# Products of two output tiles in turn, behind the in-projection of a two-layer hybrid decoder step

## What is computed

```python
def hybrid_layer(x, ...):
    z = rmsnorm(x, g_mix) @ w_in                 # 2048 -> 5632, 11 projections of 512
    ...                                          # conv module, short conv, RG-LRU, retention
    mix = concat([y_a, y_b, y_c, y_d])
    x = x + mix @ w_out                          # 2048 -> 2048
    h2 = rmsnorm(x, g_ffn)
    gpre = causal_dwconv(h2 @ w_ffn_gate, ...)   # 2048 -> 5632, width 3
    x = x + (silu(gpre) * (h2 @ w_ffn_up)) @ w_ffn_down
```

## Time and profile before

| | us |
|---|---|
| median of 3 runs | 2357.85 |
| lowest, highest | 2357.66, 2360.24 |
| the profiled execution, its own time | 2360.99 |
| its span, first to last instruction | 2359.2 |

### The profile page before, as it was taken

The page is one execution under the profiler, slowest core; times in us unless marked ns, Lnnn a source line. Parts: engine busy times, 40 slices in busy tenths (PEclk is TensorE's granted clock), DMA queues, the critical chain, the costliest instruction groups (busy, mean ns, idle before and its releaser), DMA issues.

```text
span 2359.2 us, 44193 instructions
## 1 busy us (share of the span) xinstructions
PE 2306.2 (98%) x18830; PEld 2295.7 (97%) x18830; DVE 1620.6 (69%) x2581; ACT 1016.9 (43%) x1124; POOL 0.2 (0%) x4
## 2 busy tenths in 40 slices
PE   7999989999999999999999999999999999999997
PEld 7999989999999999999999998999999999999996
DVE  7987766666666666666789867557666666666666
ACT  6433644434433433433554346444433443443444
POOL 0000000000000000000000000000000000000000
PEclk9999999999999999999999999999999999999998
DMA  7646445555555555555566554455555555555552
GB/s 273 204 167 206 143 159 185 179 188 181 181 166 195 180 182 185 182 172 188 176 201 205 166 188 153 164 179 185 181 181 186 181 171 188 178 185 188 179 180 91
DMA packets 119237, 426.07 MB, mean 181 GB/s; under 512 B 15489, under 2 KB 15745, under 8 KB 119041
## 3 DMA queue, kind: packets, MB, share of 16 engines
q1 hardware_dynamic: 111888, 407.15, 52.5%
q10 hardware_dynamic: 7152, 16.09, 1.9%
HBM read 413.71 MB, written 9.48 MB: 179 GB/s over the span
## 4 chain that ended last, share of the span: by engine, by line
PE 94%; DVE 4%; DVEq 1%; ACT 1%; issue 0%; DMA 0%; SPq 0%; ACTq 0%
PE bank L560 31%; PE bank L561 31%; PE bank L562 30%; DVE wl L772 1%; PE bank L680 1%; DMA x<-in_x_in 0%; ACT wh L254 0%; PE bank L708 0%; PE bank L673 0%; DVE x L1218 0%; DVE u L801 0%; DVE ml L862 0%; DVE x L1168 0%; DVE ssq L1016 0%; PE bank L638 0%
## 5 line engine op out<-in xcount | busy, mean ns | idle before, releaser
L254 ACT ACTIVATE wh<-raw 128x1024 fp32r<-128x1024 f32 x768 | 813.0, 1062 | 1247.0 <-PE bank L562 1226.6
L560 PE MATMUL bank<-xh,wh 128*128 128x264 f32 x4224 | 1206.9, 286 | 13.3 <-DVE wl L772 10.9
L561 PE MATMUL bank<-xl,wh 128*128 128x264 f32 x4224 | 1200.4, 284 | 0.0
L562 PE MATMUL bank<-xh,wl 128*128 128x264 f32 x4224 | 1199.4, 284 | 0.0
L772 DVE TENSOR_TENSOR wl<-raw,wh 128x1024 fp32r<-128x1024 f32 x768 | 916.9, 1220 | 36.3 <-ACT wh L254 9.3
L560 PEld LDWEIGHTS bank<-xh,wh 128*128 128x128 f32 x4224 | 799.2, 189 | 17.5 <-issue 11.5
L561 PEld LDWEIGHTS bank<-xl,wh 128*128 128x128 f32 x4224 | 799.8, 189 | 0.4
L562 PEld LDWEIGHTS bank<-xh,wl 128*128 128x128 f32 x4224 | 795.6, 188 | 0.0
L560 PE MATMUL bank<-mh,wh 128*128 128x264 f32 x1920 | 548.3, 286 | 25.5 <-DVE ml L862 15.8
L561 PE MATMUL bank<-ml,wh 128*128 128x264 f32 x1920 | 547.6, 285 | 0.0
L562 PE MATMUL bank<-mh,wl 128*128 128x264 f32 x1920 | 544.7, 284 | 0.0
(11 more groups left out here) (196 smaller groups left out, 676.3 us busy)
## 6 DMA issues: line engine op xcount, KB each, us to landing
raw<-in_weights SPq DMA_DIRECT2D x768, 512.0 KB, 4.0
s_own<-in_ret_state ACTq DMA_DIRECT2D x4, 512.0 KB, 6.3
k<-in_ret_state ACTq DMA_DIRECT2D x4, 512.0 KB, 4.5
out_new_ret_sample<-s_own ACTq DMA_DIRECT2D x4, 512.0 KB, 5.5
out_new_ret_sample<-k ACTq DMA_DIRECT2D x4, 512.0 KB, 5.3
x<-in_x_in SPq DMA_DIRECT2D x3, 528.0 KB, 9.2
dg<-in_ffn_state ACTq DMA_DIRECT2D x2, 528.0 KB, 4.4
out_new_ffn_sample<-dg ACTq DMA_DIRECT2D x2, 528.0 KB, 2.7
```

The lines of the kernel that those rows point to most:

```text
L254: act.activation(wh[:, i, :], raw[:, i, :], ACT.Copy).then_inc(hi_made, 1)
L560: pe.matmul(out, w_hi, rh, start=first, stop=False)
L561: pe.matmul(out, w_hi, rl, start=False, stop=False)
L562: return pe.matmul(out, w_lo, rh, start=False, stop=last)
```

## The change

In the output projection (g = 12 to 14), up 0 and all gate and up groups of the loop, `group` is replaced by `group_by_twos`: two tiles, in two banks, go together, block by block, each of the three products for the one and then for the other. It uses two chunks at a time (the host puts the weights in that order) and needs four chunks for the two tiles, which end together. In-projection, groups in halves and down-projections stay. The waits on `chunk_used` and the arguments of `lows_to` follow: `4 * (m // 2) + 4` chunks in place of `2 * m + 2`, and for every second tile 2 chunks more. `silu_gate` on ScalarE goes one chunk earlier in the loop, and for block 0 behind the last chunk of the plan.

```diff
--- before.py
+++ after.py
@@ -90,8 +90,11 @@
 def done(p):
 
 
+
     g, m = divmod(p, 4)
-    return 8 * g + (5 + m if g in HALVES else 2 * m + 2)
+    if g in HALVES:
+        return 8 * g + 5 + m
+    return 8 * g + (2 * m + 2 if g < G_IN else 4 * (m // 2) + 4)
 
 
 class Signal:
@@ -490,20 +493,21 @@
                          (44, h_store_par)]
                 plan += [(43, h_mix(3 + m, 12 + m, 1, u[:, m, :], "yb", m + 1)) for m in range(4)]
                 plan += [(44 + kk, lambda kk=kk: h_x(kk)) for kk in range(KT)]
-                plan += [(61, lambda: std_of(l, 1)), (64, lambda: silu_gate(l, 0))]
+                plan += [(61, lambda: std_of(l, 1))]
                 plan.sort(key=lambda item: item[0])
                 for n in range(RING, 8 * G_LOOP):
                     hi(l * CHUNKS + n)
                     while plan and done(plan[0][0]) + LEAD <= n:
                         plan.pop(0)[1]()
                 assert not plan
+                silu_gate(l, 0)
 
                 for blk in range(1, NBLK):
                     for n in range(24):
                         hi(l * CHUNKS + G_LOOP * 8 + (blk - 1) * 24 + n)
                         if 8 <= n < 12:
                             hh_of(l, blk - 1, (blk - 1) % 2, n - 8)
-                        if n == 18:
+                        if n == 17:
                             silu_gate(l, blk)
 
                 def split_next(j):
@@ -580,6 +584,26 @@
                     for f in (hooks or {}).get(m, ()):
                         f()
 
+            def group_by_twos(chunk, i, tile, rh, rl):
+
+                for m in (0, 2):
+                    for j in range(2):
+                        c = 2 * m + 2 * j
+                        pe.wait_ge(lo_made, chunk + (c + 2))
+                        for b in range(8):
+                            kk = 8 * j + b
+                            at, cols = [(i + c + n) % RING for n in range(2)], slice(b * P, (b + 1) * P)
+                            for n in range(2):
+                                if kk == 0:
+                                    pe.wait_ge(bank_empty.sem, tile + (m + n + 1))
+                                pe.matmul(bank[:, m + n, 0:T], wh[:, at[n], cols], rh[:, kk, :], start=kk == 0, stop=False)
+                            for n in range(2):
+                                pe.matmul(bank[:, m + n, 0:T], wh[:, at[n], cols], rl[:, kk, :], start=False, stop=False)
+                            for n in range(2):
+                                last = pe.matmul(bank[:, m + n, 0:T], wl[:, at[n], cols], rh[:, kk, :], start=False, stop=kk == 15)
+                                if b == 7:
+                                    last.then_inc(chunk_used.sem, 1)
+
             def group_in_halves(chunk, i, tile, rh, rl, hooks=None, before=None):
 
                 for j in range(2):
@@ -732,12 +756,12 @@
                         on("mix_lo", l, kk - 8)
                 group_in_halves(c0 + G_IN * 8, G_IN * 8, t0 + G_IN * 4, mh, ml, None, mixers_ready)
                 for g in range(G_IN + 1, G_GATE0):
-                    group(c0 + g * 8, g * 8, t0 + g * 4, mh, ml)
+                    group_by_twos(c0 + g * 8, g * 8, t0 + g * 4, mh, ml)
                 group_in_halves(c0 + G_GATE0 * 8, G_GATE0 * 8, t0 + G_GATE0 * 4, xh, xl, {1: [lambda: sum_squares(1)]},
                                 norm_ready(l * 32 + KT))
 
                 on("std", l, 2)
-                group(c0 + G_UP0 * 8, G_UP0 * 8, t0 + G_UP0 * 4, xh, xl)
+                group_by_twos(c0 + G_UP0 * 8, G_UP0 * 8, t0 + G_UP0 * 4, xh, xl)
 
                 def hidden_ready(base):
                     def f(kk):
@@ -747,8 +771,8 @@
                 for blk in range(1, NBLK):
                     i = G_LOOP * 8 + (blk - 1) * 24
                     tb = t0 + G_LOOP * 4 + (blk - 1) * 8
-                    group(c0 + i, i, tb, xh, xl)
-                    group(c0 + i + 8, i + 8, tb + 4, xh, xl)
+                    group_by_twos(c0 + i, i, tb, xh, xl)
+                    group_by_twos(c0 + i + 8, i + 8, tb + 4, xh, xl)
                     down(c0 + i + 16, i + 16, l * PAIRS + (blk - 1) * 8, (blk - 1) % 2,
                          hidden_ready(l * (4 * NBLK) + (blk - 1) * 4))
                 down(c0 + G_LAST * 8, G_LAST * 8, l * PAIRS + (NBLK - 1) * 8, 0,
@@ -1121,7 +1145,7 @@
                     p = 44 + kk
                     dve.wait_ge(chunk_used.sem, chunk_used.at(l, done(p)))
                     tt(x[:, kk, :], x[:, kk, :], bank[:, p % 4, 0:T], ALU.add).then_inc(bank_empty.sem, 1)
-                    lows_to(c0 + done(p) + LEAD)
+                    lows_to(c0 + done(p) + LEAD + (0 if kk < 4 or kk == KT - 1 else 2 * (kk % 2)))
                     if kk:
                         split_x(l, 0, kk - 1, gain(1))
                     if kk == KT - 1:
@@ -1131,7 +1155,7 @@
                 add_squares(3, S["x_sq"].at(l, 4), e)
 
                 def gate_tile(chunk, m, last=None):
-                    dve.wait_ge(chunk_used.sem, chunk + ((last or 2 * m + 2) + RING))
+                    dve.wait_ge(chunk_used.sem, chunk + ((last or 4 * (m // 2) + 4) + RING))
                     tt(q[:, m, :], bank[:, m, 0:T], rs[:, :], ALU.mult).then_inc(bank_empty.sem, 1)
 
                 def gate_conv(f0, between=lambda: None):
@@ -1150,7 +1174,7 @@
                         between()
 
                 def up_tile(chunk, blk, m):
-                    dve.wait_ge(chunk_used.sem, chunk + (2 * m + 2 + RING))
+                    dve.wait_ge(chunk_used.sem, chunk + (4 * (m // 2) + 4 + RING))
                     tt(one_tile[m % 2], bank[:, m, 0:T], rs[:, :], ALU.mult).then_inc(bank_empty.sem, 1)
                     dve.drain()
                     if m == 0:
@@ -1178,20 +1202,20 @@
                 gate_conv(0, lambda: lows_to(n_lo + 1))
                 for m in range(4):
                     up_tile(c0 + G_UP0 * 8, 0, m)
-                    lows_to(c0 + min(G_UP0 * 8 + 2 * m + 2, G_LOOP * 8) + LEAD)
+                    lows_to(c0 + min(G_UP0 * 8 + 4 * (m // 2) + 4 + 2 * (m % 2), G_LOOP * 8) + LEAD)
 
                 for blk in range(1, NBLK):
                     cb, half = c0 + G_LOOP * 8 + (blk - 1) * 24, (blk - 1) % 2
                     for m in range(4):
                         gate_tile(cb, m)
-                        lows_to(cb + 2 * m + 2 + LEAD)
+                        lows_to(cb + 4 * (m // 2) + 4 + 2 * (m % 2) + LEAD)
                         if m:
                             h_low(blk - 1, half, m - 1)
                     h_low(blk - 1, half, 3)
                     gate_conv(blk * 4, lambda: lows_to(n_lo + 1))
                     for m in range(4):
                         up_tile(cb + 8, blk, m)
-                        lows_to(cb + 10 + 2 * m + LEAD)
+                        lows_to(cb + 8 + min(4 * (m // 2) + 4 + 2 * (m % 2), 8) + LEAD)
                     for j in range(8):
                         down_pair(cb + 16, j)
                         lows_to(cb + 17 + j + LEAD)
...
```

More of the change, by code:

```diff
@@ L1269, with put @@
     for l in range(DEPTH):
-        def put(w, first, count, rows=None):
+        def put(w, first, count, rows=None, by_twos=True):
             nonlocal at
             c = _chunks(np, w, first, count, rows)
+            n = 0
             if at % CHUNKS // 8 in HALVES:
+                n = 8
                 c[:8] = c[:8].reshape(4, 2, P, CHUNK).transpose(1, 0, 2, 3).reshape(8, P, CHUNK)
+            if by_twos:
+                c[n:] = c[n:].reshape(-1, 2, 2, P, CHUNK).transpose(0, 2, 1, 3, 4).reshape(-1, P, CHUNK)
             weights[at:at + len(c)] = c
@@ L1279 @@
         for g in range(G_IN):
-            put(w, g * W_GROUP, 4)
+            put(w, g * W_GROUP, 4, by_twos=False)
         put(a["w_out"][l], 0, KT, OUT_ROWS)
@@ L1285 @@
             if blk:
-                put(a["w_ffn_down"][l][(blk - 1) * 512:blk * 512], 0, KT)
-        put(a["w_ffn_down"][l][(NBLK - 1) * 512:], 0, KT)
+                put(a["w_ffn_down"][l][(blk - 1) * 512:blk * 512], 0, KT, by_twos=False)
+        put(a["w_ffn_down"][l][(NBLK - 1) * 512:], 0, KT, by_twos=False)
     par = np.zeros((DEPTH, P, HEADS, N_PAR_IN), np.float32)
```

## The result

The changed kernel takes 2418.01 us (four runs, 2413.98 to 2420.39) against 2359.01 for the kernel before on the same chip: a ratio of 1.0249 [1.0231, 1.0267], 59 us slower. The forecast of 2402 has the sign and the waits right. It is 16 us short, because the interval between products, which it left unchanged, grew. The time lies outside the 2391 to 2413 that the bounds of the interval gave, and inside the range as it was widened to 2380 to 2421. The profiled execution took 2420.39 us, its span is 2418.6, 59.4 more than before.

The account below looks back on a forecast made before the run. TensorE, busy 98% of the span, was taken as the bound, through the product interval and new waits. Waits of 42.5 + 1.6 = 44.1 us, interval unchanged, gave 2405.1, or 2402 against the median; range 2391 to 2413, widened to 2380 to 2421.

Parts of the forecast that it names:

- The 22 waits: Third pair of ten gate groups and the first paired output group, both layers: TensorE waits 1.93 us each, 42.5 us.
- five terms: One wait: tile start 0.20, low start 0.35, low made 1.22, TensorE resuming 0.05, slower first interval 0.11; 1.93 us.
- The interval: Between the 9,216 reordered products: unchanged at 120.8 ns; bounds 122.0 (11 us more) and 111 (88 us less).
- repeated operand: In the paired products: two neighbours reading the same moving tile save nothing, so the interval stays 120.8 ns.
- Rival D: Pair before the down-projection misses its slack, or the new read order costs 11 us: 2413 to 2425, chance 0.07.
- main forecast: Whole kernel: 2402 us, with the interval between products within 1.2 ns of 120.8, chance 0.76.
- Up group 0: First up group: VectorE is just late, TensorE's second product is delayed 0.8 us, 1.6 in two layers.
- What was said to cost nothing: Later up tiles, `silu_gate`, the down-projection's start, raw weight loads and the host's reordering: no added time.
- 0.7 us of slack: Down-projection start: the bank pair is empty at 855.25, TensorE's third chunk is due at 855.99, so no wait.
- Rival A: Paired products: alternating banks or the shared moving tile shortens the interval towards 111 ns, giving 2314 us; chance 0.09.
- Rival B: At the new waits: TensorE's clock falls, 22 x 1.7 = 37 us more, 2439 us; chance 0.04.
- Chunks 6 and 7: Chunk ring in a gate group: they may be made 5.8 us before use at 17.4; no bound by throughput.

Follow-up runs that it names:

- the order by chunk: The changed kernel, but within a pair one chunk's 24 products come before the other's, tiles and chunks still handed over in pairs: 2404.02 us, 1.0187 of before.

## Why the prediction came out as it did

**The 22 waits: right in place, number and size.** Each of the five terms can be read off. The next start would have been at 825.65 + 5.88 = 831.53; `gate_tile(0)` starts 0.21 later (said: 0.20), the low 0.35 behind it (0.35), it takes 1.22 (1.22), TensorE goes on at 833.36, 0.05 after its end (0.05). The fifth term was 0.11 for the first interval; the next pair is 0.05 longer. Together 1.88, where 1.93 was said: 41.3 us, not 42.5. In the order by chunk it was 1.93.

**The interval: the term that was mis-sized.** It was put at 120.8 ns, unchanged, with +1.2 and -9.6 as bounds. It came to 5.87 us a pair on average, 122.4 ns: 0.91 us in the three output groups, 5.86 in the blocks, 0.29 in up group 0, a layer 7.06, in all 14.1 us in place of 0, and 0.3 ns outside the bound. The upper bound came from the right row, the down-projection's 122.0, but for no reason that was known. The step that failed is the one on the repeated operand. "No row shows a repeated moving tile" was true, and the text took the row of these groups, in the old order, for it. Yet the down-projection was the one place in the trace where the reads come in another order, and it is slower. Rival D had this as "the new order of reads costs as the down-projection's does (+11)", in a case that had 0.07: the price was nearly right, the chance too small. Its condition for the main forecast, an interval within 1.2 ns of 120.8 (chance 0.76), was not met; the time fell into the range because the range had been widened for D and B.

**Up group 0: right.** TensorE starts late at up 0 by 0.56 and loses 0.27 more in it besides its interval. On VectorE, the low of its second chunk and the second gate tile, then TensorE:

```profile
433.83 1.22 DVE L796 TENSOR_TENSOR wl<-raw,wh 128x1024 fp32r<-128x1024 f32 x1
434.96 0.42 DVE L1159 TENSOR_TENSOR q<-bank,rs 128x264 f32<-128x264 f32 x1
...
435.14 0.69 PE L599 MATMUL bank<-xh,wh 128*128 128x264 f32 x2 [0.37 <-issue]
```

The low ends at 435.05, and the first product starts at 435.14; the second can't start before the gate tile's end at 435.38. The wait for two lows stands ahead of the first product, so part of the delay lies there, where the prediction put all of it at the second. 0.83 a layer against 0.8.

**What was said to cost nothing: right.** Up tile 0 was forecast at 43.3 in the block's time; it is at 863.29 - 819.83 = 43.5:

```profile
863.29 0.43 DVE L1178 TENSOR_TENSOR tmp<-bank,rs 128x264 f32<-128x264 f32 x1
```

No wait stands at the start of a down-projection in the loop, nor in an up group, and the ten blocks are accounted for without one: 10 x 1.88 + 5.86 = 24.7 against 24.64. The rival that put a miss of the 0.7 us of slack there fell.

**Rival A fell, and by a test of its own.** With the waits removed the pairs are still slower than before, and one bank or two makes no difference. The estimate of 112.5 ns that the prediction took from the Trainium skill (TensorE: Matmul & The Clock Gate, section "Back-to-back issue gap") was not seen at 264 columns in any arrangement: 120.0 was the least. The same section of the Trainium skill gives this formula for an isolated product and says that it does not hold for a stream of weight loads and products, so by it a gap between estimate and trace is no surprise; no run here shows an isolated product.

**Rival B: wrong place, a small part of its price.** None of the 22 waits is followed by a lower clock (1.00 in 831.30 to 839.20), as the earlier trace rows had it for a wait of this length. But a half clock of 3.4 us came in behind the longer wait of the last down-projection, twice, 3.1 us, which the prediction had nowhere: it looked only at new waits, not at what an old one might do in the new kernel.

**Two slips without weight.** Chunks 6 and 7 may be made from 5.8 us on, which is 11.6 us before their use at 17.4 and not 5.8; that makes the conclusion, no bound by throughput, safer. And the chances of the rivals and those of the last line differ by 0.01 (A has 0.09 and then 0.10).

**The sum.** 41.3 + 14.1 + 1.7 + 3.1 = 60.2 us, and 60.3 were found up to the last product. Of the 16 us by which the forecast's 44.1 was short of that, 14 are the interval and 3 the clock, less 1 for the waits. The medians are 59.0 apart; 2402 is 16 short of 2418 as well since it stood on a median of 2357.85, 1.2 under the 2359.01 of the comparison.

## What to carry to other kernels

When tiles are finished in pairs, the engine that makes the next operands is released in pairs too: look at what stands in its in-order queue behind the first wait for a finished tile, and make one operand more ahead of it. That was 41 of 60 us by the trace, and three constants took the waits away (36 us by the medians, as another wait grew). An order of products that is equal in number and shape is not equal in time: here the same products cost up to 6% more or less by where the moving operand starts, so such a term needs a bound from the nearest row that reads in another order, even when its cause isn't known.

## What the runs showed of the chip that was not expected

- The interval of 264-column products depends on where the moving operand starts. For starts 32 bytes apart, counted from the start of `xh`: 120.0 ns at 0, 64, 192 and 224 bytes past a multiple of 256, 121.7 at 160, 122.2 at 32, 123.3 at 128, 126.7 at 96. A high and a low tile at different places are slower (121.1 to 121.9) than at the same (120.8). A shift of both by 16 bytes changes it too (121.4).
- It isn't proportional to the columns: with starts at 0, 120.0 at 264, 118.7 at 260, 120.0 at 256 and 115.0 at 248, and 111.7 for 200, 160 and 128 alike. Between 200 and 128 columns something that doesn't depend on them sets the time; what it is was not tested.
- Alternating between two accumulation banks costs and saves nothing: 707.12 us for ten blocks with either.
- A wait of TensorE of 2.64 us in a row of otherwise equal work is followed by half clock for 3.4 us in one kernel and by none in another, and in one kernel (other widths) in the second layer (clock 0.50 in 2295.20 to 2298.60) and not in the first (1.00 in 1142.50 to 1149.00).
